# Splitting the output weights and the first tile's head norms in the last head's score phase, the router on x that is not yet normalised, first weights loaded in the setup

## What is computed

```python
def attn_output(o, g, wo, lam_init):
    o = rmsnorm(o, g) * (1.0 - lam_init)          # per head of 128 columns
    return o.reshape(b, n, ATTN_WIDTH) @ wo
...
    xs = xs + gs1 * ms                            # residual, gate per column; ms from either mixer
    hs = adaln(xs, norm2_g[l], ss2, cs2)          # rmsnorm(x)*g*(1 + scale) + shift
...
    aff = jax.nn.softmax((h @ w_router).astype(jnp.float32), axis=-1)
    g, idx = lax.top_k(aff.T, cap)                # the tokens of each expert
```

## Time and profile before

| quantity | value |
|---|---|
| median of 3 runs | 3611.03 us (3610.76 to 3611.32) |
| profiled run, device time | 3609.34 us |
| span of the profiled execution | 3607.6 us |
| granted PE clock, mean | 0.947 of full speed |
| busy share PE, DVE, ACT, POOL | 89%, 47%, 22%, 9% |
| setup | 0 to 70.8 us |
| attention | 71.7 to 868 us |
| mixer and route, layer 0 | 871.5 to 1102.5 us |
| experts, layer 0 | 1103.6 to 2245 us |
| pooling mixer | 2246 to 2330 us |
| mixer and route, layer 1 | 2331.2 to 2467.4 us |
| experts, layer 1 | 2468 to 3575 us |

### The profile page before, as it was taken

The page is one execution under the profiler, slowest core; times in us unless marked ns, Lnnn a source line. Parts: engine busy times, 40 slices in busy tenths (PEclk is TensorE's granted clock), DMA queues, the critical chain, the costliest instruction groups (busy, mean ns, idle before and its releaser), DMA issues. The chain is left out here.

```text
span 3607.6 us, 60425 instructions
## 1 busy us (share of the span) xinstructions
PE 3221.1 (89%) x23898; PEld 3079.2 (85%) x23898; DVE 1700.5 (47%) x3000; ACT 779.5 (22%) x1798; POOL 334.5 (9%) x426
## 2 busy tenths in 40 slices
PE   5999999997866999999999997275999999999995
PEld 2888888896756999999999996165999999999995
DVE  4666666666565344344444433875233233233232
ACT  3555555555210100110110011120110110110111
POOL 2000000000100100010010011430010010010011
PEclk8999999999877999999999998587999999999997
DMA  5111111112347788788888872166788788788683
GB/s 195 34 50 50 50 50 50 45 30 85 117 152 261 269 307 302 255 308 303 278 284 307 298 261 81 42 229 217 239 289 291 239 290 291 239 289 291 239 282 117
DMA packets 420433, 722.28 MB, mean 200 GB/s; under 512 B 15969, under 2 KB 340226, under 8 KB 420386
## 3 DMA queue, kind: packets, MB, share of 16 engines
q1 hardware_dynamic: 396194, 669.12, 52.9%
q0 software_dynamic: 15200, 38.94, 4.4%
q10 hardware_dynamic: 8992, 13.63, 1.4%
HBM read 673.40 MB, written 48.23 MB: 200 GB/s over the span
## 5 line engine op out<-in xcount | busy, mean ns | idle before, releaser
L1453 PE MATMUL bank<-ex_xT,ring 128*128 128x144 f32 x11264 | 1392.8, 287 | 15.6 <-issue 8.4
L1453 PEld LDWEIGHTS bank<-ex_xT,ring 128*128 128x128 f32 x11264 | 1386.0, 190 | 23.4 <-issue 23.4
L1470 PE MATMUL bank<-ex_hid,ring 128*128 128x144 f32 x5632 | 699.2, 286 | 0.0
L1470 PEld LDWEIGHTS bank<-ex_hid,ring 128*128 128x128 f32 x5632 | 692.7, 190 | 0.0
L1492 ACT ACTIVATE ex_ge<-bank 128x432 f32<-128x432 f32 (+1 forms) x128 | 64.1, 501 | 1301.5 <-PE bank L1453 1301.5
L1555 DVE RECIPROCAL ex_t<-ex_t 128x432 f32<-128x432 f32 (+1 forms) x128 | 336.4, 2628 | 4.5
L1554 DVE TENSOR_SCALAR ex_t<-ex_ge 128x432 f32<-128x432 f32 (+1 forms) x128 | 46.9, 366 | 607.2 <-ACT ex_ge L1492 607.2
L1574 DVE TENSOR_SCALAR ex_yeC<-bank,valC 128x128 f32<-128x128 f32 x32 | 11.2, 351 | 548.7 <-PE bank L1484 548.7
L1500 ACT ACTIVATE ex_yT<-bank,modc 128x128 f32<-128x128 f32 x256 | 95.3, 372 | 766.9 <-PE bank L1470 766.9
L550 PE MATMUL bank<-whh,hTh 128*128 128x384 f32 x576 | 200.9, 349 | 15.4 <-DVE whl L856 15.4
L837 DVE TENSOR_REDUCE nm<-bank 128x1 f32<-128x1152 f32 x144 | 176.5, 1235 | 76.8 <-PE bank L598 76.8
(11 more groups left out here) (224 smaller groups left out, 3176.1 us busy)
## 6 DMA issues: line engine op xcount, KB each, us to landing
ring<-in_expert_w_gate SPq DMA_DIRECT2D x96, 1536.0 KB, 8.7
ring<-in_expert_w_up SPq DMA_DIRECT2D x96, 1536.0 KB, 12.4
ring<-in_expert_w_down SPq DMA_DIRECT2D x96, 1536.0 KB, 12.2
ring<-in_expert_w_gate SPq DMA_DIRECT2D x32, 1024.0 KB, 6.2
ring<-in_expert_w_up SPq DMA_DIRECT2D x32, 1024.0 KB, 8.7
ring<-in_expert_w_down SPq DMA_DIRECT2D x32, 1024.0 KB, 18.6
ex_wm<-in_w_mod SPq DMA_DIRECT2D x16, 1536.0 KB, 10.5
wraw<-in_attn_wqkv SPq DMA_DIRECT2D x64, 192.0 KB, 3.2
```

The source lines that it names most:

```text
L1453: last = nc.tensor.matmul(bank[:, banks[j % 2], f * CAP:(f + 1) * CAP], wv[:, c, f * P:(f + 1) * P], xT[:, c], start=(c == 0), stop=(c == ...
L1470: last = nc.tensor.matmul(bank[:, YB[m // 3], (m % 3) * CAP:(m % 3 + 1) * CAP], wv[:, q, m * P:(m + 1) * P], hid[:, f], start=(f == 0), st ...
```

## The change

**Setup.** The nine small loads are issued by ACT. SP starts with the modulation matrix. Behind its last load SP waits until PE is done with that matrix and loads head 0's attention weights and the rotary tables into its place; attention no longer loads them.

**Last head.** As soon as `wraw` is free, SP loads the output weights into it (six pieces, and two more when the first two are split). In turns 2 to 9 of the last head's score phase ACT makes their high part and in turns 3 to 7 and 9 DVE the remainder. SP stores `ot` of tiles 0 and 1 early and loads the heads' outputs of these two tiles; DVE and POOL make tile 0's head norm in turns 8 and 9. The stage no longer ends with a wait for its last stores: SP of the next stage waits before it loads tile 2, and the cached keys and values are waited for at the end of the program.

**Mixer and route, both layers.** The product, the gate and the residual are done in halves of 512 columns. PE transposes x itself, not the normalised x; ACT copies the transpose to `h2`, and the norm gain is multiplied into the router weights beforehand (`wrg`). The logits are (x @ wrg) * root + bias, where the bias is the shift times the router weights (`bias_mm`). In layer 0 the eight router products of an earlier tile stand one by one between the heads of the first half product, and head norms run two tiles ahead of the product. The context tokens' affinities go to rows 64 to 79 of the same table, so the two extra rounds fall away, and the last MATCH_REPLACE8 too. The table's two fills go to POOL.

```diff
@@ setup, SP and ACT @@
-                    sp.dma_start(ident[:], a["ident"]).then_inc(s_id, 16)
...
+                    sp.wait_ge(cols_T, 2)
+                    sp.wait_ge(row_mm, NT)
+                    for i in range(4):
+                        load_w(sp, 0, i)
...
+                    act.dma_start(ident[:], a["ident"]).then_inc(s_id, 16)
...
@@ attention, SP @@
-                    store_o(H - 1)
-                    sp.wait_ge(S["kv_out"], 32 * H + 1)
-                    sp.wait_ge(S["o_out"], 32 * H + 1)
+                    sp.wait_ge(S["o_evac"], TT * (H - 1) + 2 + 1)
+                    sp.dma_start(lat[:, 0:2], ot[:, 0:2]).then_inc(o_out, 16)
+                    for i in range(NRAW, H):
+                        sp.wait_ge(S["wo_lo"], i - NRAW + 1)
+                        load_wo(i)
+                    sp.wait_ge(o_out, 32 * (H - 1) + 16 + 1)
+                    load_o(sp, 0)
+                    load_o(sp, 1)
...
@@ attention, ACT and DVE, turn n of a head @@
+                            if not more and 2 <= n < 2 + H:
+                                wo_high(n - 2)
...
+                            if not more:
+                                if 3 <= n <= 7:
+                                    wo_low(n - 3)
+                                if n == 8:
+                                    head_squares(dve, 0)
+                                if n == 9:
+                                    wo_low(5)
+                                    wo_low(6)
+                                    wo_low(7)
+                                    head_scale(dve, 0)
...
@@ mixer, PE @@
+                        for c in range(H):
+                            for k, (x, y) in enumerate(((oTh, woh), (oTh, wol), (oTl, woh))):
+                                last = nc.tensor.matmul(bank[:, b, :], x[:, t % 2, c], y[:, c, b * 512:(b + 1) * 512],
+                                                        start=(c == 0 and k == 0), stop=(c == H - 1 and k == 2))
+                            if router_t is not None:
+                                router(router_t, c)
...
@@ mixer, DVE, a half of the residual, and the order of a turn @@
+                        dve.wait_ge(S["mm_done"], 2 * t + b + 1)
+                        if b == 0:
+                            dve.wait_ge(S["bc_ok"], NB)
+                            dve.wait_ge(x_in_s[t % 2], 16 * (t // 2 + 1))
+                            if not attn:
+                                dve.wait_ge(S["xb_ok"], t + 1)
+                        y = bank[:, PB[t % 2] + b, :]
+                        nc.vector.tensor_tensor(y, y, gA[:, cond_of[t], b * 512:(b + 1) * 512], ALU.mult).then_inc(S["xu"], 1)
...
+                        if s < TT:
+                            residual(s, 0)
+                        if attn and s == 1:
+                            logit_bias()
+                        if 2 <= s <= TT + 1:
+                            logits(s - 2)
+                        if attn and s + 1 < TT:
+                            oT_low(s + 1)
+                        if attn and s + 2 < TT:
+                            head_scale(dve, s + 2)
+                        if 2 <= s <= TT + 1:
+                            affinity(s - 2)
+                        if s >= 3:
+                            affinity_row(s - 3)
                         if s < TT:
...
+                            residual(s, 1)
```

More of the change, by code:

```diff
@@ L1045, in product, with product_p @@
+                    def product_p(t, b):
+                        if t >= 2:
+                            pe.wait_ge(S["x_half"], 2 * t - 3 + b)
+                        for g in (2 * b, 2 * b + 1):
+                            for c in range(2):
+                                last = nc.tensor.matmul(bank[:, PB[t % 2] + b, (g % 2) * GROUP:(g % 2 + 1) * GROUP],
+                                                        pT[:, 2 * g + c, t], pw[:, g, c], start=(c == 0), stop=(c == 1))
                         last.then_inc(S["mm_done"], 1)
@@ L1071, in _, with bias_mm @@
+                    def bias_mm():
+                        pe.wait_ge(S["rw_ok"], 1)
+                        for cond in range(2):
+                            for c in range(DC):
+                                last = nc.tensor.matmul(bank[:, 6, cond * E:(cond + 1) * E], ones[:], wrs[:, cond, c],
+                                                        start=(c == 0), stop=(c == DC - 1))
+                        last.then_inc(S["lb_mm"], 1)
                     if attn:
                         turn_o(0)
+                        rows_mm(0)
+                    else:
+                        for b in range(NB):
+                            rows_mm(b)
+                        bias_mm()
+                        pe.wait_ge(S["w_in"], 16)
@@ L1073, in _ @@
                     for s in range(TT + 3):
+                        r = s - 2 if 2 <= s <= TT + 1 else None
                         if s < TT:
-                            product(s)
+                            if attn:
+                                product_o(s, 0, r)
+                            else:
+                                product_p(s, 0)
+                        if r is not None and not (attn and s < TT):
+                            for c in range(DC):
+                                router(r, c)
@@ L1092, in _ @@
+                    last.then_inc(S["top_mm"], 1)
                     pe.wait_ge(S["anti_in"], 16)
```

544 lines of the change are left out of this document (294 added, 250 removed).

## The result

The changed kernel takes **3572.15 us** (median of 4 runs, 3567.24 to 3573.36), the kernel before, measured beside it, 3610.9 (4 runs, 3608.36 to 3611.32): 0.9892 of it, with a 95% interval of 0.9874 to 0.9909. That is 38.8 us less where 42.1 were forecast, inside the range. The profiled run took 3571.72 us (span 3569.9).

A forecast was written before the change was run, and what follows sets the result against it. PE bounds the untouched expert stages and, at clock 0.90, layer 0's mixer loop; a DVE, ACT and POOL chain sets layer 1's mixer. Terms sum to -42.1 us from 3609.34; forecast 3568.9 on the median's scale, range 3555 to 3585.

The forecast's parts named there:

- Setup, -3.3: Setup: SP starts the modulation matrix 3.54 us earlier, small loads go out on ACT; 3.3 us saved, nothing if loads delay PE.
- attention's start, -7.2: Start of attention: weights already loaded, so of PE's 9.27 us wait only split, remainder and hand-over (2.0) stay; 7.2 us saved.
- Last head, +0.3: Attention's last head: added weight splits and head norm mostly fit idle gaps; costs 0.3 us, bounds 0 and +2.1.
- Stage change, -2.1: Attention's end to layer 0's mixer: landing of the last stores no longer waited for; 2.1 us saved, bounds 0 and -3.5.
- Up to the product, -11.6: Layer 0's mixer before its first product: only cold transpose, first gate row and hand-overs remain, 5.7 instead of 17.26 us.
- The loop, -17.7: Layer 0's mixer loop: full clock and no remainder wait, 134.8 instead of 152.5 us; 17.7 us saved.
- rival (1): Layer 0's mixer: the clock still falls in each tile, costing 15 us, total 3584; chance 0.13.
- Tail, -6.1: Layer 0, last product to top-k: 11.8 instead of 17.9 us; 6.1 us saved.
- Top-k, -2.9: Top-k: the two context rounds and the last replacement go; 2.9 us saved.
- Layer 1's mixer, +8.5: Layer 1's mixer: DVE's turn grows from 6.86 to 8.9 us, less tail and top-k gains; costs 8.5, bounds +6 and +11.
- (2): Layer 1's mixer: the turn does not grow, as POOL or the halves overlap; 16 us less, total 3553; chance 0.12.
- (3): Layer 1's mixer: PE loses its clock and enters the chain, +14 us, total 3583; chance 0.07.

The follow-up runs named there:

- the experiment: Changed kernel with the nine small setup loads issued by SP ahead of the modulation matrix again, early weight loads kept: 3573.85 us.
- the last version: Changed kernel with layer 1's mixer reordered, its bias later, bias in 8 matmuls of 32 columns, two last-head remainders on POOL: 3544.21 us.

## Why the prediction was right, step by step

- **Setup, -3.3, and attention's start, -7.2:** measured together -8.9. The small loads land at 8.89 instead of 5.32, though the last is issued only 0.36 later (4.34 instead of 3.98), so of the 3.54 us that SP gains PE loses most, waiting for `silu`. The bound of the text (they share the DMA engines with the matrix) was named, and the value taken was too near the other end: 1.8 by the experiment. That the sharing is what delays them fits these times, but no run tried it alone. The second term was off by about 1.
- **Last head, +0.3:** 0 measured (up to +1.0 in other profiles with the same code), score turns of 5.77. The cover was there.
- **Stage change, -2.1:** -1.3. What is late next had been taken for a short hand-over; it is DVE's three remainders and the head's scaling, to 860.3. The landing alone is worth 1.
- **Up to the product, -11.6:** -12.7, since gate rows and transposes overlap better than the 5.7 counted.
- **The loop, -17.7:** -17.3, and 2.3 more in the seven of ten profiles with the halves in which the fall behind the bias doesn't come (loop 132.9 to 133.2). The forecast's size was right, its reason was not: it took full clock because the narrow block is broken up. With the router in one block, and with the whole block between the halves, the clock stayed at 1.00 all the same. What keeps it, with the block in its old order, is that no wait follows: the wait for the remainder, priced at 0.4 by itself, was the key to the other 1.7. The halves, which the prediction counted, hide that wait, so the clock came out right for a reason that it didn't have. That the sum is off by only 0.4 is luck too: the fall behind the bias (2.3) was not foreseen, and the rest of the loop is 1.8 shorter than the 134.8 counted.
- **The rule on transposes** of the Trainium skill ("TensorE: Matmul & The Clock Gate", Part 4: PE-mode transpose), beside rival (1) with its 3584: the clock stayed at 1.00 with all transposes and a router block in one place and no idle time behind. So here transposes by themselves don't cost the clock; the rule may still be a part of why a block with idle time does, which no run shows.
- **Tail, -6.1:** -5.5; the router ran at half clock (3.53) as feared. **Top-k, -2.9:** -2.9 in layer 1; in layer 0 0.8 of it went in what follows.
- **Layer 1's mixer, +8.5:** +9.3 (12.2 - 2.9). The turn was forecast at 8.9 and is 8.73. Two smaller terms were mis-sized: the start, +0.4 forecast, is +2.2, with a second gate row at half clock and the bias matmuls ahead of the product; and the tail gains 3.8, not 5.1. Against them the eight turns, some +16 in the sum, are +13.8 (68.74 - 54.90).
- **Rivals:** (2), a turn that doesn't grow, fell with the wait of 31.9 us. (3), PE in the chain, is absent from the changed kernel, though its clock fell as feared (0.87 in the loop); it came true in four turns of the run with both halves in a row. (4), weight loads, and (5), a mixer that still waits, show no sign.

No row of the ledger is off by more than 1.6 us. Within the loop and within layer 1's mixer errors of about 2 us cancel, as told above, and there the agreement is better than the reasoning. On layer 1 the prediction took the new wait as given; that it could be taken away again with the rest kept is what the last version shows.

## What to carry to other kernels

- Where PE waits for the second part of an operand, cut the product in two, so that half of it covers the other engine's work; with the wait went a clock that fell behind it, and the loop became 24 us shorter where the waits were 12.7.
- An engine works in order: a new wait holds all that is queued behind it. Put it directly ahead of the operation that needs it, and the cheap independent work ahead of it: 8.73 us a turn became 7.0 and 6.0 with the same operations (PE's two halves were put in a row with it, and that was not tried apart). Look at the other engines' queues as well: the softmax moved on DVE alone stayed in the chain through ACT.
- Work moved into another stage's gaps still has an end: look which engine finishes that stage last, here DVE.

## What was not expected of the hardware

- The clock falls behind a narrow block with idle time after it and not behind the same block without: loops of 157.0 and 133.0 us. With another order in the block 0.79 us of idle time cost it in one tile only.
- The 32 bias matmuls of 16 columns, with PE busy, are followed by a stretch at 0.50 in layer 0 in three of the ten profiles with the halves, and in both with whole products: 2 to 3 us that come and go from run to run. At layer 1's start, after PE's long idle time, the stretch up to the first sum of squares takes 25.0, 26.7 or 28.2 us in kernels that don't differ there, by how many gate rows pass before the clock rises (two or three) and whether it falls again behind the bias.
- Some operations of DVE and POOL shut each other out. A remainder on POOL beside DVE's squares made these 2.89 us instead of 1.22, and a 128x1 operation took 1.23 where it takes 0.22 elsewhere. The Trainium skill ("SBUF — State Buffer", Who interferes with whom) says that a VectorE operation with two inputs in SBUF and a GpSimd operation that reads SBUF exclude each other for a whole instruction; both rows agree, even the tiny one.
